# Streaming 32 experts' weights through a ring: every second 2 MB load of 22 experts begun by ScalarE on its own queue instead of by SyncE

## The reference, cut to what matters

```python
gu = xb @ w_gate_up[e] + b_gate_up[e]          # (tokens,1024) @ (1024,2048)
gate = jnp.minimum(gu[:, :D_FF], SWIGLU_LIMIT)
up = jnp.clip(gu[:, D_FF:], -SWIGLU_LIMIT, SWIGLU_LIMIT)
h = (up + 1.0) * gate * jax.nn.sigmoid(SWIGLU_ALPHA * gate)
return h @ w_down[e] + b_down[e]               # (tokens,1024) @ (1024,1024)
```

## Time and profile before

| | |
|---|---|
| median of 3 runs | 1041.1 us (1040.77 to 1042.49) |
| the profiled execution's own time | 1040.72 us |
| its span (first to last instruction) | 1039.0 us |
| PE busy | 984.9 us, 95% of the span |
| DMA queue of SyncE (q1) | 417.08 MB, 95.5% of 16 engines' span |
| DMA queue of ScalarE (q10) | 1.08 MB, 0.4% |
| ScalarE busy | 121.7 us, 12% |
| granted clock of TensorE | 0.997 of full speed over the whole span |

### The profile page before, as it was taken

The page is one execution under the profiler, slowest core; times in us unless marked ns, Lnnn a source line. Parts: engine busy times, 40 slices in busy tenths (PEclk is TensorE's granted clock), DMA queues, the critical chain, the costliest instruction groups (busy, mean ns, idle before and its releaser), DMA issues.

```text
span 1039.0 us, 11031 instructions
## 1 busy us (share of the span) xinstructions
PE 984.9 (95%) x4587; PEld 416.1 (40%) x4587; DVE 214.7 (21%) x467; ACT 121.7 (12%) x192; POOL 8.5 (1%) x27
## 2 busy tenths in 40 slices
PE   9999999999999999999999999898999989899996
PEld 6684534343433333343434343333334333333432
DVE  2234431212121111121212121121012121120121
ACT  2352200101010000010101010010001010000002
POOL 0011000000000000000000000000000000000000
PEclk9999999999999999999999999999999999999999
DMA  9967589999999999999999999999999999999994
GB/s 321 413 249 295 200 356 430 430 426 429 426 429 390 430 426 430 425 430 427 430 428 429 429 428 430 428 428 428 428 428 430 428 429 429 428 428 427 427 426 189
DMA packets 34388, 418.57 MB, mean 403 GB/s; under 512 B 4221, under 2 KB 4761, under 8 KB 9657
## 3 DMA queue, kind: packets, MB, share of 16 engines
q1 hardware_dynamic: 32720, 417.08, 95.5%
q10 hardware_dynamic: 1640, 1.08, 0.4%
HBM read 417.10 MB, written 1.05 MB: 402 GB/s over the span
## 4 chain that ended last, share of the span: by engine, by line
PE 68%; DMA 24%; DVE 4%; issue 2%; ACT 1%; SPq 0%; DVEq 0%; ACTq 0%
PE bank L1140 57%; DMA ring<-in_w_gate_up_dram 20%; PE acc L1140 10%; DMA ring<-in_w_down_dram 4%; DVE area L981 1%; DVE area L978 1%; DVE area L917 1%; ACT wpool L604 1%; PE bank L1506 1%; DVE sel L691 0%; DMA xres<-in_x_dram 0%; PE bank L1168 0%; ACT late L468 0%; ACT late L652 0%; DVE masks L896 0%
## 5 line engine op out<-in xcount | busy, mean ns | idle before, releaser
L1140 PE MATMUL bank<-ring,area 128*64 128x512 f32 (+1 forms) x1936 | 434.8, 595 | 20.3 <-DMA ring<-in_w_gate_up_dram 20.3
L1140 PEld LDWEIGHTS bank<-ring,area 128*64 128x64 f32 (+1 forms) x1936 | 137.7, 138 | 309.8 <-issue 265.8
L1140 PE MATMUL bank<-ring,wpool 128*64 128x512 f32 x912 | 204.1, 599 | 7.4 <-ACT wpool L604 4.5
L975 DVE TENSOR_SCALAR area<-bank 128x512 f32<-128x512 f32 x32 | 22.1, 692 | 460.7 <-PE bank L1140 460.7
L1140 PEld LDWEIGHTS bank<-ring,wpool 128*64 128x64 f32 x912 | 63.7, 137 | 125.8 <-issue 117.1
L600 ACT ACTIVATE bank<-area 128x512 f32<-128x512 f32 x32 | 19.3, 602 | 494.1 <-DVE area L975 494.1
L1140 PE MATMUL bank<-masks,xres 128*128 128x128 f32 x504 | 67.3, 287 | 2.3 <-DVE masks L896 0.3
L1140 PEld LDWEIGHTS bank<-masks,xres 128*128 128x128 f32 x504 | 61.8, 196 | 17.5 <-issue 16.4
L998 DVE COPY wide<-bank 64x512 f32<-64x512 f32 x30 | 20.8, 694 | 185.7 <-PE bank L1140 185.7
L613 ACT ACTIVATE wide<-bank 64x512 f32<-64x512 f32 x30 | 17.7, 591 | 239.9 <-PE bank L1140 239.9
L1140 PE MATMUL bank<-bias,sel 64*128 64x512 f32 x128 | 38.0, 641 | 0.0
(11 more groups left out here) (178 smaller groups left out, 430.9 us busy)
## 6 DMA issues: line engine op xcount, KB each, us to landing
ring<-in_w_gate_up_dram SPq DMA_DIRECT2D x119, 2048.0 KB, 26.5
ring<-in_w_down_dram SPq DMA_DIRECT2D x58, 2048.0 KB, 31.1
area<-in_w_gate_up_dram SPq DMA_DIRECT2D x6, 2048.0 KB, 14.4
area<-in_w_down_dram SPq DMA_DIRECT2D x4, 2048.0 KB, 14.4
late<-in_w_gate_up_dram SPq DMA_DIRECT2D x3, 2048.0 KB, 18.9
ring<-in_w_in_dram SPq DMA_DIRECT2D x8, 512.0 KB, 10.0
ring<-in_w_in_dram SPq DMA_DIRECT2D x4, 1024.0 KB, 19.0
ring<-in_w_out_dram SPq DMA_DIRECT2D x4, 1024.0 KB, 16.6
```

The source lines that it names most:

```text
L975: v.tensor_scalar(gatec, gbank[:], LIMIT, None, ALU.min).then_inc(gc, 1)
L1140: return t.matmul(o, l, r, start=start, stop=stop, skip_group_check=True)
```

## The change

The loads c2, c6 and c10 of experts 8 to 29 (66 transfers of 2 MB) are begun by ScalarE on its queue. SyncE begins c0, c4 and c8 of the same experts; experts 0 to 7, 30 and 31 stay with SyncE. The condition that a load waits for is the same on either engine. In ScalarE's program c6 and c10 of expert e+1 stand behind the sigmoid of expert e, and c2 of expert e+2 behind the copy of expert e's result. ScalarE's loop now has four experts to a turn, so that the slots are constants of the program. `rows_of` has moved out of the SyncE program, unchanged.

```diff
+        ACT_LOADS = (2, 6, 10)
...
             def load_expert(e, m0):
 
                 for c in range(0, PER_EXPERT, 2):
+                    if c in ACT_LOADS:
+                        continue
 
                     sp.wait_ge(chunks_used, e * PER_EXPERT + (c + 1) - (RING - 1))
                     load_two(e, c, slot_of(m0 + c))
...
+            def load_two(e, c, m0):
+
+
+                act.wait_ge(chunks_used, e * PER_EXPERT + (c + 2 - RING))
+                src = rows_of(e, c, 2)
+                s = slot_of((m0 + c) % PER_BODY)
+                dst = pair_place(s).rearrange("p (s f) -> p s f", s=src.shape[1])
+                act.dma_start(dst, src).then_inc(chunk_in[s // 2], 16)
+
+            def load_next(e, r):
+
+                for c in ACT_LOADS[1:]:
+                    load_two(e + 1, c, (r + 1) * PER_EXPERT)
+
+            def load_after_next(e, r):
+
+                load_two(e + 2, ACT_LOADS[0], (r + 2) * PER_EXPERT)
+
...
-            def fast_expert(e, r, gains=False):
+            def fast_expert(e, r, gains=False, next_=False, after=False):
                 fast_sigmoid(e)
+                if next_:
+                    load_next(e, r)
                 if gains:
                     last_gains()
                 fast_hidden(e)
                 act.wait_ge(chunks_used, (e + 1) * PER_EXPERT)
                 lo = (r % 2) * SLOTS
                 a.activation(ypair[lo:lo + SLOTS, 0:HALF], BY[0:SLOTS, :], ACT.Copy).then_inc(y_lo, 1)
+                if after:
+                    load_after_next(e, r)
...
-                with act.Fori(0, NE // 2 - 2) as q:
+                with act.Fori(0, FIRST // 2 - 1) as q:
                     for r in range(2):
                         fast_expert(q * 2 + r, r)
-                fast_expert(NE - 4, 0)
+                for r in (2, 3):
+                    fast_expert(FIRST - BODY + r, r, next_=(r == 3), after=True)
+                with act.Fori(0, NLOOP - 1) as i:
+                    for r in range(BODY):
+                        fast_expert(i * BODY + (FIRST + r), r, next_=True, after=True)
+                fast_expert(NE - 4, 0, next_=True)
                 fast_expert(NE - 3, 1, True)
```

More of the change, by code:

```diff
@@ L291, in down_w, with rows_of @@
             return place(slot)[:, lo:lo + HALF]
+        def rows_of(e, c, n):
+            if c < UP_CHUNKS:
+                src = rows["wgu"][bass.ds(e * D + (c // 2) * 2 * P, 2 * P), :]
+                return src.rearrange("(p s) f -> p s f", s=2)[:, c % 2:c % 2 + n, :]
+            c -= UP_CHUNKS
+            src = rows["wd"][bass.ds(e * F + (c // 2) * 4 * P, 4 * P), :]
+            return src.rearrange("(p s) f -> p s f", s=4)[:, 2 * (c % 2):2 * (c % 2) + 2 * n, :]
+        ACT_LOADS = (2, 6, 10)
         def head_rms(j):
@@ L317, in _ @@
                              ).then_inc(wout_in[c], 16)
[L319 to L326, removed]
             def load_two(e, c, s):
@@ L613, in fast_expert, with all_tokens @@
                 a.activation(ypair[lo:lo + SLOTS, 0:HALF], BY[0:SLOTS, :], ACT.Copy).then_inc(y_lo, 1)
-            with act.If(crowded):
[L616 to L627, removed]
+                if after:
+                    load_after_next(e, r)
+            def all_tokens(e, r=0, next_=False, after=False):
+                for tt in range(TT):
+                    for hf in range(2):
+                        n = e * 4 + (2 * tt + hf + 1)
+                        act.wait_ge(gc_ok, n)
+                        a.activation(BG[:], gatec, ACT.Sigmoid, scale=ALPHA).then_inc(sig_ok, 1)
+                        act.wait_ge(hT_ok, n)
+                        a.activation(hidT_all[:, 4 * hf:4 * hf + 4, :],
+                                     BG[:].rearrange("p (j t) -> p j t", j=4),
+                                     ACT.Copy).then_inc(hT_c, 1)
+                        act.wait_ge(hT_c, n)
+                if next_:
+                    act.wait_ge(chunks_used, (e + 1) * PER_EXPERT)
+                    load_next(e, r)
+                if after:
+                    act.wait_ge(chunks_used, (e + 1) * PER_EXPERT)
+                    load_after_next(e, r)
+            with act.If(crowded):
+                with act.Fori(0, FIRST - 2) as e:
+                    all_tokens(e)
+                for r in (2, 3):
+                    all_tokens(FIRST - BODY + r, r, r == 3, True)
+                with act.Fori(0, NLOOP - 1) as i:
+                    for r in range(BODY):
+                        all_tokens(i * BODY + (FIRST + r), r, True, True)
+                all_tokens(NE - BODY, 0, True)
+                with act.Fori(0, BODY - 1) as e:
+                    all_tokens(e + (NE - BODY + 1))
                 last_gains()
```

## The result

| | before | changed |
|---|---|---|
| median of 20 runs | 1041.26 us | 1044.29 us |
| ratio, 95% interval | | 1.0031 (1.0023 to 1.0040) |
| profiled execution: span | 1039.0 us | 1042.2 us |
| granted clock over the span | 0.997 | 0.992 |

The change makes the kernel slower by 0.31%, some 3.2 us. That is inside the stated range, but beyond the 0.2% that bounds "no change": the likeliest case, 1041.6 us, did not happen. One execution of the kernel before, at 1462.4 us, is a slow one and is left out of the ratio.

The account below looks back on a forecast made before the run. Bytes over the DMA rate, plus pauses and PE's work after the last landing, set the end. Order 0.1, dip 0.3, c2 0.1 and mixing 0 add 0.5 us: 1041.6 us forecast, range 1037 to 1060.

Parts of the forecast that it names:

- the stated range: Whole kernel: 1037 to 1060 us, leaving out the better half of rival 3, the top of rival 1 and all of rival 2.
- the likeliest case: Whole kernel: 1041.6 us, within 2.1 us of the time before; chance 0.45.
- What bounds the kernel: Whole run: the end is bytes over the rate, plus DMA pauses, plus PE's work after the last landing.
- rivals 1 and 3: Both queues at work: switching costs +9 to +27 us (rival 1, chance 0.30), or overlap gains 4.5 to 10 us (rival 3, 0.13).
- The 26 ns per packet: Small packets at the start, two queues against one; over 1056 packets per engine an upper bound of +27 us.
- rival 2: DMA engines serve SyncE's queue first, so c10(29) lands near 1004 us: 30 us more, about 1072 us; chance 0.05.
- ScalarE at no cost: ScalarE's program: two issues, 1.1 to 1.3 us, fit the 2.32 us gap between sigmoid and hidden copy; cost nothing.
- The order of arrival: Experts 8 to 29: equal sharing makes pairs land together, ScalarE's load 4.9 us later; c6(29) near 959.8 instead of 954.9.
- The slack at the end: Experts 30 and 31: PE's old DMA waits, together 4.79 us, absorb the 4.9 us delay; 0.1 us is left.
- the pause behind the dip: After the ring shrinks from 22 to 16 places, near 337 us: later c6(8) leaves DMA engines idle, 0.3 us taken.
- rival 4: At c6(29): delay exceeds one transfer as packets are shared in coarser pieces; two to four us more, 1044 us; chance 0.07.

Follow-up runs that it names:

- the later ring: 12 experts ahead of the loop instead of 8, so the ring shrinks from 22 to 16 places later: kernel before 1039.39 us, changed kernel 1040.01 us.
- the late c6 on one queue: Kernel before, all loads on SyncE's queue, but c6 of experts 8 to 29 begun behind c8, waiting for c10's count: 1043.15 us, ratio 1.0017.
- filling the idle time: Changed kernel plus 8 unread matmuls of ones ahead of the wait for c6: in experts 28 and 29 1045.03 us, in 29 alone 1044.12 us.
- the run with c2 and c10 alone: Changed kernel, but ScalarE begins only c2 and c10, and c6 goes back to SyncE at its old time: 1043.54 us, ratio 1.0025.

## Why the prediction was right or wrong

**What bounds the kernel:** right. The stretches of 30 us and more without a pause that were read have 426 to 431 GB/s, and taking 2.4 us of pause out of the kernel before took 2.1 us off its time.

**Mixing costs or gains time (rivals 1 and 3):** both wrong. 428 GB/s with two queues against 428 with one. The 26 ns per packet that I drew from the small tables at the start are not paid by 16 KB packets; the value that I took, 0, was the right end of the bounds.

**One queue is preferred (rival 2):** wrong. The pairs land together, and a lightly filled queue overtakes at half of the rate. The round by packets that the Trainium skill describes (DMA: Bandwidth & Descriptors, Queues, rings and completion order) agrees with the counts, 253 packets of ScalarE's queue against 256 of SyncE's in 18 us; whether an engine changes queues after each single packet no view here shows.

**ScalarE at no cost:** right (2.92 us from sigmoid to hidden copy, before and after). That c6(8) waits for the sigmoid's end was wrong, without harm: it was begun at 333.01, not near 334.3.

**The order of arrival, 4.9 us at c6(29):** right in size for this kernel, and in part by luck. The pairs (c2, c4) and (c6, c8) are in the landings, and the share is equal. But the prediction took it for granted that an equal share makes neighbours land together. With c6 ahead of the sigmoid, and with the later ring, the share is equal as well and they land 4 to 6 us apart. Wrong in a detail: PE's waits did not move to c2, c6 and c10 but to c6 alone, mostly 1.3 or 2.3 us at a time.

**The slack at the end, "of 4.9 us, 0.1 us is left":** this is the step that failed. The waits of 4.79 us were read rightly, and they were used up; but I let the delay fill them to the last tenth and then put hardly anything on top. On top came
- the later grid of all landings, 1.8 us at c8(29), of which the pause behind the dip is 1.0 us. I had taken 0.3 us, from bounds of 0 to 1.2. I had looked for a gap ahead of c6(8)'s bytes only; the first part lies at 330 to 332 us, ahead of those of c8(8), which before were bridged by c6(8), begun near 326 us;
- 0.4 us between c8(29) and c6(29);
- 1.70 us for the 16 matmuls of c6(29) at the lower clock, a term that I did not have.

4.9 + 1.8 + 0.4 + 1.7 = 8.8 us, the measured 8.76. Less 4.79 us of waits 4.0 are left, of which 3.3 reached the end. The other 0.7 us are at the same four places: a group that follows without a wait begins while the one before is still being counted. The down matmuls at 1015.58, for example, begin 6.87 us after the group before them, which began at 1008.71; in the kernel before it was 9.35 us, of which 2.31 are the wait and 7.04 the group. The time that came true is that of **rival 4**, "each us over 4.9 reaches the end; two to four us, 1044 us", to which I had given 0.07 because I could think only of coarser sharing as its cause. I should have seen that a forecast which ends 0.1 us before an edge, with delays that can only add, has most of its chance beyond the edge. And that 1044.3 us lies inside the stated range is no merit of this sum: the range was as wide as it was because of rivals 1 and 3.

**What stays open:** how much of the 3 us the clock carries. Without the fall the sum would give some 1.6 us, near what the late c6 on one queue cost, but that run had the fall in its profile too, and filling the idle time moved the fall instead of removing it. That a late order costs time without any fall behind it, the run with c2 and c10 alone shows: 2.6 us.

## What to carry to other kernels

A second DMA queue adds no rate to engines that are already busy; it reorders. Two queues with work shared the engines equally in the stretches counted here, whatever their depth, so a transfer on the lighter queue overtakes, and two that begin together both arrive when the second would. Before splitting an ordered stream, compare how late a transfer may be with the waits behind its last use, and read the order of the landings in the trace. When loads go into an engine's own program, their place there sets that order. c6 put where its condition becomes true took the whole loss away with one ring (1042.04 us), and with the other it made the kernel 5.9 us slower than c6 behind the sigmoid (1045.89 against 1040.01 us): no place is right by itself.

If a ring shrinks during a run, let it do so when the queue is long enough to bridge the gap: that one constant is worth 2.1 us, and the kernel before with it has the lowest median of this study.

## What was not expected of the hardware

Two queues that start unevenly stay uneven: 33 against 25 us from issue to landing at equal bytes, from expert 16 (c0 32.4 us, c2 23.1) to expert 28 (33.1 and 23.7).

And the granted clock fell for short stretches, mostly in the kernels in which PE's waiting comes in few long pieces. Before, 19 waits of PE for gate and up weights, most of them 1.2 us, 20.3 us in all, and a clock of 0.997; changed, 14 waits, 2.3 us the longest, 24.9 us in all, and 0.992. The other kernels at 0.996 and 0.997 (c6 ahead of the sigmoid; the later ring with one queue, and with the change) have 17 to 26 waits of at most 1.6 to 2.2 us, and of these three only the later ring with one queue has a fall between 200 and 1030 us, the one shown above; those at 0.986 to 0.993, the one-queue kernel with late c6 among them, have 8 to 17, the longest 2.3 to 4.1 us. A fall at the end costs 1.5 to 3.0 us (16 matmuls 5.35 us instead of 3.65, 64 matmuls 16.92 instead of 13.95), but not every long wait is followed by one: 2.31 us ahead of 903.28 in the changed kernel was not. The spread of the changed kernel's runs is wider too, 1042.1 to 1047.2 us over 20, against 1039.4 to 1043.3 before.
